# Five places of their own for the transform's weight pieces in a two-block network on one core

## The reference, cut to what matters

```python
u = rms_norm(h, norm_w[l]) @ w_in[l]
f_in, f_gate, p_in, p_gate, c_q, c_kv, k_r, a_gate = jnp.split(u, split_idx, axis=-1)
y_f = fourier_mix(f_in, fourier_w[l])      # fft2 over tokens and channels, real part, then a small product
y_p = pool_mix(p_in, pool_w[l], pool_scale[l])   # window means of 2, 4, 8, 16 tokens
y_a = mla_mix(c_q, c_kv, k_r, ...)         # attention
mix = jnp.concatenate([y_f * silu(f_gate), y_p * silu(p_gate), y_a * silu(a_gate)], axis=-1)
h = h + mix @ w_out[l]
```

## Time and profile before

| | |
|---|---|
| median of 3 runs | 3913.2 us (3906.98 to 3915.26) |
| profiled execution, its own time | 3908.01 us |
| its span | 3906.3 us, 50688 instructions |
| TensorE matmul busy | 3694.0 us, 95% |
| GpSimd busy | 1083.5 us, 28% |
| VectorE, ScalarE busy | 1695.6 us, 43%; 1269.0 us, 32% |
| mean granted TensorE clock | 0.982 |
| DMA of weights | 228 issues of 512 KB, 4.3 us from issue to landing in the middle |

### The profile page before, as it was taken

The page is one execution under the profiler, slowest core; times in us unless marked ns, Lnnn a source line. Parts: engine busy times, 40 slices in busy tenths (PEclk is TensorE's granted clock), DMA queues, the critical chain, the costliest instruction groups (busy, mean ns, idle before and its releaser), DMA issues. The chain is left out here.

```text
span 3906.3 us, 50688 instructions
## 1 busy us (share of the span) xinstructions
PE 3694.0 (95%) x20618; PEld 3257.6 (83%) x20618; DVE 1695.6 (43%) x3158; ACT 1269.0 (32%) x2893; POOL 1083.5 (28%) x794
## 2 busy tenths in 40 slices
PE   6999998999999999999899999989999999998998
PEld 5887887878887788788788888778988998998898
DVE  5434554433335453355523334564344345334433
ACT  3112443033341221144403344222245422234541
POOL 2633222312112354322222121235310013531012
PEclk9999999999999999999999999999999999999999
DMA  3121111411104311211141101432110022210012
GB/s 115 38 73 65 36 33 52 151 33 44 44 30 161 111 50 65 71 33 33 44 151 44 35 34 38 160 109 70 44 36 16 24 89 76 68 46 23 13 43 98
DMA packets 84617, 243.88 MB, mean 62 GB/s; under 512 B 10656, under 2 KB 24224, under 8 KB 84384
## 3 DMA queue, kind: packets, MB, share of 16 engines
q1 hardware_dynamic: 84384, 240.64, 18.2%
HBM read 190.07 MB, written 50.53 MB: 62 GB/s over the span
## 5 line engine op out<-in xcount | busy, mean ns | idle before, releaser
L2691 POOL TENSOR_SCALAR Whi<-stage 128x1024 fp32r<-128x1024 f32 (+5 forms) x268 | 274.7, 1025 | 2069.2 <-DMA stage<-wstream 1280.0
L1388 PE MATMUL pj<-Hhi,Whi 128*128 128x512 f32 x1640 | 662.4, 404 | 10.8 <-DVE Hlo L2125 3.6
L1388 PE MATMUL pj<-Hhi,Wlo 128*128 128x512 f32 x1640 | 645.1, 393 | 0.0
L1388 PE MATMUL pj<-Hlo,Whi 128*128 128x512 f32 x1640 | 643.6, 392 | 0.0
L2693 POOL TENSOR_TENSOR Wlo<-stage,Whi 128x1024 fp32r<-128x1024 f32 (+5 forms) x268 | 622.0, 2321 | 22.4
L1388 PEld LDWEIGHTS pj<-Hhi,Whi 128*128 128x128 f32 x1640 | 311.9, 190 | 81.3 <-ACT PT L1828 6.6
L1388 PEld LDWEIGHTS pj<-Hhi,Wlo 128*128 128x128 f32 x1640 | 310.7, 189 | 67.4
L1388 PEld LDWEIGHTS pj<-Hlo,Whi 128*128 128x128 f32 x1640 | 311.8, 190 | 59.6
L1388 PE MATMUL pS<-Hhi,Whi 128*128 128x512 f32 x792 | 315.5, 398 | 17.4 <-DVE Hlo L2125 9.9
L1388 PE MATMUL pS<-Hlo,Whi 128*128 128x512 f32 x792 | 313.3, 396 | 0.0
L1388 PE MATMUL pS<-Hhi,Wlo 128*128 128x512 f32 x792 | 313.1, 395 | 0.0
(11 more groups left out here) (429 smaller groups left out, 7471.0 us busy)
## 6 DMA issues: line engine op xcount, KB each, us to landing
stage<-wstream SPq DMA_DIRECT2D x228, 512.0 KB, 4.3
merged<-Mb SPq DMA_DIRECT2D x32, 512.0 KB, 2.9
Mb<-merged SPq DMA_DIRECT2D x32, 512.0 KB, 4.1
gates<-tmp SPq DMA_DIRECT2D x48, 256.0 KB, 2.2
TH<-gates SPq DMA_DIRECT2D x24, 512.0 KB, 6.0
xres<-X SPq DMA_DIRECT2D x16, 520.0 KB, 2.9
xr<-xres SPq DMA_DIRECT2D x16, 520.0 KB, 4.1
X<-xT SPq DMA_DIRECT2D x16, 256.0 KB, 7.7
```

Source lines behind the costliest of these rows:

```text
L1388: x = pe.e.matmul(ps, w[a][:, v.koff + k * P:v.koff + k * P + P], moving(v.of, b, k, v.t0, v.n), start=k == 0 and i == 0, stop=k == v.K - ...
L2691: pool.e.tensor_scalar(upper, stage, 1.0, 0.0, ALU.mult, ALU.add).then_inc(*pool.tick("whi", c))
```

## The change

The eight transform weights of a layer no longer go through the three places of `m.W`. They have a ring of five places of their own, `m.D`, in the bytes of `m.Y`. Each weight carries its ring and its place (`place`), and the weight whose place it takes (`before`). The numbering is changed with it: two transform weights are asked for ahead of the second pooled input's weight, six behind it. The first two hang on the unit `f[0][2]`, the next three on the first unit of `p[1]`, and the load of two more on `pool0`; splits into the first five places wait for `y_free`.

```diff
+ND = 5
+    m.D = [(at(f"Dhi{i}", y0 + 6336 * i, [P, 786], F32R), at(f"Dlo{i}", y0 + 6336 * i + 3168, [P, 786], F32R)) for i in range(ND)]
...
+        self.rings, self.place, self.before, self.sent, self.split_at, self.d_free = ([], []), [], [], {}, {}, {}
...
-            at = max(at, self.first[c].id if c < NR else behind[self.used_at[c - NR]])
+            b = self.before[c]
+            free = self.first[c].id if c < NR else self.split_at.get(c, 0) if b is None else behind[self.used_at[b]]
+            at = max(at, self.sent.get(c, free))
             self.units[at].setdefault("loads", []).append(c)
-            self.units[self.split[c].id if c < NR else at].setdefault("splits", []).append(c)
+            self.units[self.split[c].id if c < NR else max(at, free, self.split_at.get(c, 0))].setdefault("splits", []).append(c)
...
     def weight(self, key):
+        c, d = len(self.weights), key[0] == "dft"
+        ring, size = self.rings[d], ND if d else NR
         self.weights.append(key)
-        return len(self.weights) - 1
+        self.place.append((d, len(ring) % size))
+        self.before.append(ring[-size] if len(ring) >= size else None)
+        ring.append(c)
+        return c
...
         self.add(p[0][2])
+        dw = [("dft", part, kc, piece) for kc in range(2) for part in range(2) for piece in range(2)]
+        dc = [self.weight(x) for x in dw[0:2]]
...
         self.run(p[1])
+        dc += [self.weight(x) for x in dw[2:]]
+        for j, c in enumerate(dc):
+            if j < ND:
+                self.d_free[c] = list(self.y_free)
+                self.sent[c] = self.split_at[c] = (f[0][2] if j < 2 else p[1][0]).id
...
         u = self.put("pool0", l=l, p_ready=p_ready[0], folded=("lo", fold, 5), a_ready=a_ready)
+        for c in dc[ND:ND + NS]:
+            self.sent[c] = u.id
...
-                    u["c"] = self.weight(u.dkey)
+                    u["c"] = dc[dw.index(u.dkey)]
...
-        w = m.W[u.c % NR]
+        w = m.D[order.place[u.c][1]]
...
-        stage, (upper, lower) = m.stage[c % NS][:, 0:n], (w[:, 0:n] for w in m.W[c % NR])
+        d, i = order.place[c]
+        stage, (upper, lower) = m.stage[c % NS][:, 0:n], (w[:, 0:n] for w in (m.D if d else m.W)[i])
         pool.wait_ge(("w_in", c))
-        pool.wait_ge(("wused", c - NR))
+        pool.wait_ge(("wused", order.before[c]))
+        for x in order.d_free.get(c, ()):
+            pool.wait_ge(x)
```

More of the change, by code:

```diff
@@ L1384, in proj @@
             for v in group:
-                w, ps = m.W[v.c % NR], m.pj[v.bank][:, 0:v.n]
+                w, ps = m.W[order.place[v.c][1]], m.pj[v.bank][:, 0:v.n]
                 pe.wait_ge(("wlo", v.c))
@@ L1575, in values_in @@
     def values_in(u):
-        w, ps = m.W[u.c % NR], m.pj[u.bank]
+        w, ps = m.W[order.place[u.c][1]], m.pj[u.bank]
         pe.wait_ge(("wlo", u.c))
```

## The result

| | before | after |
|---|---|---|
| median | 3907.12 us (20 runs, 3899.8 to 3924.1) | 3916.14 us (20 runs, 3908.8 to 3923.2) |
| ratio after to before | | 1.0018 (95% interval 1.0009 to 1.0026), +7.0 us |
| profiled execution, its own time | 3908.01 us | 3920.96 us |
| its span, mean granted clock | 3906.3 us, 0.982 | 3919.2 us, 0.978 |
| TensorE matmul busy | 3694.0 us | 3708.1 us |

The ratio is that of the comparison, not the quotient of the two medians (1.0023). The change costs a few microseconds. The lines of the code lie 21 to 24 lower than before: L1409 is the projections, L1562 `amix`, L1578 `dft`, L2565 the fold, L2715 and L2717 the splits, now with outputs `Dhi`, `Dlo` for the new places.

A forecast was written before the change was run, and what follows sets the result against it. TensorE, busy 95% of the span, was taken as the bound. First layer +5.6 - 1.4 - 2.3 - 0.75 = +1.15 us, second +5.6 - 1.5 - 1.9 - 0.7 = +1.5; +2.6 on 3913.2 gives 3915.8 us, range 3908 to 3924.

The forecast's parts named there:

- Part 1, the stall: Start of `p[1]`: its weight comes late, TensorE waits 3.5 us plus 1.5 us slow start; `p[1]` ends 5.1 us later.
- Part 2, the fold: VectorE's fold beside GpSimd's splits at `p[1]`: held until 2679.8, so `amix` moves by 5.6 us.
- my lower end: Start of `amix`: if the fold isn't held, it moves by `p[1]` alone, 4.7 us.
- the 4 us that I had named as a sign of being wrong: Start of `amix`: a move of less than 4 or more than 8 us would make the prediction wrong.
- rival B: At `p[1]`: the stall alone, VectorE not delayed beyond `p[1]`; +0.8 us, 3914.0; chance 0.26.
- rival C: VectorE's fold held by GpSimd's splits at nearly each step, both layers; +9.4 us, 3922.6; chance 0.12.
- Part 3, what is won: Transform and first gate: waits for weights go, 1.4 + 2.3 us first layer, 1.5 + 1.9 second, plus half the slow starts.
- The wait of 1.4 us ahead of the sixth to seventh transform weight goes: Inside the transform: splits no longer wait for the place of a weight three before; 1.4 us won, first layer.
- 3.1 us become 0.8: First gate, first layer: weight ready in time, only the bank late; 2.3 us won.
- the 2.3 us ahead of the fifth unit stay: Fifth transform unit: the 2.3 us wait remains, since VectorE's `Fy` must empty the bank.
- Rival A: `p[1]` isn't held, its weight arrives in time; everything won, nothing paid: 10 us, 3903.2; chance 0.04.
- D: First gate: a split of the ring's second turn is late, the gate waits as before; +8.2 us, 3921.4; chance 0.04.

The follow-up runs named there:

- c4: Kernel after the change, unchanged, profiled a third time; single execution 3904.64 us.
- e1: Kernel after, but the weight of `p[1]` asked for first again, the first five transform weights split at `p[1]`'s first unit; ratio to before 1.0036, +14 us.
- e2: Kernel after, but the splits of the third to fifth transform weights moved behind `pool0`'s sums; ratio to before 1.0014, +5.5 us.
- c5: Kernel before the change, unchanged, profiled a fourth time; single execution 3915.39 us.
- c1: Kernel before the change once more, no edit; ratio to before 0.9999 (0.9988 to 1.0010).
- c3: Kernel before the change, unchanged, profiled a third time; single execution 3905.89 us.
- e3: Kernel after, with the weight of `p[1]` first and the third to fifth transform weights' splits behind `pool0`'s sums; ratio to before 0.9994, -2.3 us.
- e4: e3 plus the seventh transform weight's split waiting for `pool0`'s last VectorE instruction, `zlo`; ratio to before 0.9991 (0.9980 to 1.0001).
- e7: The same kernel as e4 in a second comparison; ratio to before 0.9992 (0.9979 to 1.0004).
- c2: Kernel after the change once more, no edit; ratio to before 1.0010 (1.0001 to 1.0019), +3.9 us.

## Why the prediction came out as it did

The forecast was +2.6 us in a "same" of 0.2%, 3915.8; the measurement is +7.0 and +3.9 us (3916.14 median), still inside 0.2% and inside the range. The absolute time matches better than it deserves: over 20 runs the kernel before has its median 6 us lower, at 3907.1, than over the three on which I built (3913.2). What counts is the difference, and that was too small by 2.4 us in the stretch (+5.0 instead of +2.6). That so small a difference came out near its forecast is luck in part: two of its terms were off by more, the cost by 2.8 us and the gain by 4.2 us over the two layers.

- **Part 1, the stall.** Forecast: a load sent near 2658.6, split done at 2665.7, 3.5 us of wait and 1.5 of slow start. Measured: load sent at 2659.2 (behind 1.89 us of `Dlo`), split done at 2666.1, 3.3 and 2.4 us of wait (2.3 to 3.3 in six stretches, mean 2.8). The slow start came in three of the six, both layers of this profile and c4's second, and cost 1.4 to 1.5 us; in the other three the clock stayed at 1.00. So the stall cost 3.5 us a layer in the mean, not 5.0 (the prediction's 5.1 is a slip: 3.5 + 1.5 = 5.0). A slow start, first layer:

```profile
2667.00:2670.00 3.00, 3.00 (x13) 3.00 (x12) 2.57 (x2) 0.40 (x1) 2.92 (x3) 0.54 0.25 89
```

- **Part 2, the fold.** Right in kind. Forecast end 2679.8, measured 2678.7, level with `p[1]`'s; `amix` moved by 3.8 to 4.5 us in six stretches (mean 4.2) where I had 5.6, and my lower end was 4.7. In two of the six it moved by less than the 4 us that I had named as a sign of being wrong (3.8 and, just, 3.99). The fold was the later of the two in five, by 0.6 to 0.9 us and once 2.2, and not at all in the first layer of the profile shown. e1 and e2 show that either cause alone moves it by about the same, so of forecast and rival B, B was the nearer on the size, though the fold is the later one mostly, as forecast; rival C is out. The Trainium skill, SBUF — State Buffer, section "SBUF: two separate sides", has VectorE and GpSimd exclude each other on their shared ports; the rows bear it out three times, 2.36 us for 0.69 in `A`, 4.67 for 2.50 in the `zlo` pair, and GpSimd's `Dlo` of 780 columns 2.69 us where a `Wlo` of 786 took 1.88.
- **Part 3, what is won: the step that failed.** "The wait of 1.4 us ahead of the sixth to seventh transform weight goes" and "3.1 us become 0.8" are both seen in the profile after. Against the execution from which they were read even the sum comes out, 136.9 - 134.2 = +2.7 us for a forecast of +2.6, though by a cost and a gain that were each 1 us or more a layer too large. But that execution was the kernel before at its slowest in this stretch, 134.2 us against a mean of 131.5 over four. Its waits for weights, and its slow start at the gate, exist only in some of the executions; in three of eight stretches the fifth unit waits 4.3 or 4.7 us for `Fy` instead, a wait that the change doesn't touch. I had taken "the 2.3 us ahead of the fifth unit stay" for a constant, and in the unchanged kernels it is 2.3 or 4 to 5 by the clock at the transform's start. By the table the transform with the gate's wait gained 1.5 us a layer (23.0 to 21.5), not the 3.6 of the prediction; the slow start at the gate 0.7 (14.6 to 13.9), as I had put it.
- **One term was missing.** `amix` ran slow once in six stretches of the kernel after (12.3 us) and never in eight of before: 0.5 us a layer in the mean.

Per layer then: +4.2 + 0.5 - 1.5 - 0.7 = +2.5, two layers +5.0. The prediction had +5.6 - 3.6 - 0.7 = +1.3 each. A too large cost and a much too large gain cancelled in part.

Rival A is out (the stall is there in all six stretches), D too (the gate never waits for a weight). The rest of the 12.9 us between the two profiled spans, 10.2 us, lies outside the stretch, where the two programs do the same work, and isn't the change's: span less stretch is 3772.1, 3767.4, 3773.5 and 3780.6 us in the four executions of before (mean 3773.4), and 3782.3, 3772.4 and 3767.4 in the three of after (mean 3774.0). The longer ones have the lower mean clock: 0.978 in c5 and in the profile after, 0.984 and 0.983 in c1 and c4. A slow phase of the first layer's attention, some 205 us behind the gate's start, that the profile after has and the profile before hasn't, is in c1 and c3 too, which are the kernel before.

**What stays open.** Why the clock is low behind the same wait of 1.5 us in some executions and not in others. And why e3, which pays only 0.4 us a layer ahead of `amix`, gains at most 0.2%: its stretch (133.3 us) holds an `amix` of 12.4 us in the first layer and a transform of 25.2 in the second, so part of its prize went back to the clock and to the fifth unit's wait, 3.9 us there; one profile can't say how often.

## What to carry to other kernels

A wait in one profile is a sample: where it stands behind a place at which the clock may or may not fall, take three or four profiles of the unchanged kernel and count in how many the wait is there, before its length is booked as a gain. More places to split into don't help a load whose staging place isn't free; adding weights ahead of one that was just in time costs a load and a split (here 2.3 to 3.3 us of wait). And idle time can cost more than its length: here 1.4 to 1.5 us or nothing ahead of the wide matmuls of `p[1]`, 5.5 ahead of the narrow ones of `amix`. The wait was longer in the second case, 5.1 us against 2.3 to 3.3, so that the narrowness does it isn't shown.

## What the runs showed of the hardware that was not expected

- Behind a wait of 5.1 us, `amix`'s 128-column matmuls ran at a granted 0.50 for their whole length, 14.5 us instead of 9.0, in both layers of e1; the clock rose in the transform behind them (0.97 in the last stretch shown). Behind waits of 0.8 us `amix` was slow, 12.4 us, in one of six stretches of e3, e4 and e7, and behind one of 2.2 us in c2 (12.3 us).
- The same program, with the same wait of 1.46 us ahead of the transform, began it at 0.52 in one execution and at 1.00 in another (c1).
- A slow `amix` was followed by a fast transform: 19.7 to 20.5 us up to the gate in the four stretches that had one (e1's two, c2's second, e3's first), 20.9 us and more in all others. So the price of a slow phase isn't simply added; whether it is the early one that spares the later isn't shown.
- GpSimd's splits hold VectorE's instructions that read two tiles from SBUF, but not `Alo`, whose one operand is a PSUM bank: in e2 two `Alo` that began within a `Dlo` (2672.02 beside 2671.32 to 2672.63, 2674.99 beside 2674.47 to 2676.32) took 0.69 us, as they do with none beside.
